# Expert loops of a two-layer network unrolled, with the token gather inside the loop and more weight slots

## The reference

```python
def expert_choice_ffn(h, w_router, w1, w3, w2):          # h: (1, 256, 1024)
    cap = (EC_CAPACITY_FACTOR * T) // N_EXPERTS          # 32 tokens per expert, 16 experts
    aff = softmax(h @ w_router)
    gate, idx = top_k(swapaxes(aff, 1, 2), cap)
    xe = h[bidx, idx]
    hid = silu(einsum('becd,edf->becf', xe, w1)) * einsum('becd,edf->becf', xe, w3)   # w1, w3: 1024 x 1024 per expert
    ye = einsum('becf,efd->becd', hid, w2) * gate        # w2: 1024 x 1024 per expert
    return zeros_like(h).at[bidx, idx].add(ye)
for l in range(2):
    h2 = rms_norm(x, norm_ffn[l]) * (1 + sc2) + sh2
    x = x + g2 * expert_choice_ffn(h2, ...)
    if l == 0:                                           # the context stream, with the same weights
        xc = xc + g2c * expert_choice_ffn(hc2, ...)
```

## Time and profile before

| | us |
|---|---|
| median of 3 runs (2080.01 to 2083.17) | 2082.44 |
| the profiled execution | 2084.03 |
| its span, first to last instruction | 2082.2 |
| PE busy in the span | 1763.1 (85%) |
| DVE, ACT, POOL busy | 605.1, 333.9, 124.7 |
| longest part of the chain that ended last | L603 on PE 55%, DMA of in_moe 19% |
| mean granted PE clock | 0.943 |

### The profile page before, as it was taken

One profiled execution on the slowest core, in us unless ns is written; L12 is line 12 of the kernel. 1 busy time (PEld: TensorE's weight loads), 2 busy tenths in 40 slices (PEclk: granted clock), 3 DMA queues, 4 the chain that ended last, 5 costly groups with the idle time before them and its releaser, 6 DMA issues.

```text
span 2082.2 us, 22735 instructions
## 1 busy us (share of the span) xinstructions
PE 1763.1 (85%) x9074; PEld 857.0 (41%) x9074; DVE 605.1 (29%) x1359; ACT 333.9 (16%) x717; POOL 124.7 (6%) x176
## 2 busy tenths in 40 slices
PE   6999999899999998899998888989998655555655
PEld 3844544444444575433332222346564322222222
DVE  2157827742200583421111111130343100010101
ACT  2112222211101462110000000021331000000000
POOL 0000112340100000000000000000000000000000
PEclk9999999999999999999999999999999888787877
DMA  8241238775422102339999999941313899999996
GB/s 322 101 162 67 96 144 302 268 277 218 161 81 81 41 1 81 122 125 430 429 429 428 428 428 428 428 208 52 136 74 128 370 428 428 428 429 428 428 428 279
DMA packets 39058, 537.57 MB, mean 258 GB/s; under 512 B 4330, under 2 KB 4714, under 8 KB 6612
## 3 DMA queue, kind: packets, MB, share of 16 engines
q1 hardware_dynamic: 37860, 530.85, 61.6%
q0 software_dynamic: 1136, 5.88, 0.8%
HBM read 535.66 MB, written 1.05 MB: 258 GB/s over the span
## 4 chain that ended last, share of the span: by engine, by line
PE 58%; DMA 21%; issue 13%; DVE 4%; POOL 2%; ACT 1%; DVEq 1%; POOLq 1%; SPq 0%; ACTq 0%
PE bank L603 55%; DMA mem<-in_moe 19%; PE bank L613 2%; DVE mem L1277 1%; DMA mem<-in_w_ada 1%; DVEq L1274 1%; PE bank L610 1%; POOL mem L2234 0%; DMA mem<-in_ada_w 0%; POOL mem L2222 0%; POOLq L2223 0%; POOL mem L2225 0%; DVE mem L1720 0%; ACT mem L1874 0%; POOL mem L2216 0%
## 5 line engine op out<-in xcount | busy, mean ns | idle before, releaser
L603 PE MATMUL bank<-mem 128*32 128x256 f32 (+9 forms) x8390 | 1662.0, 504 | 280.0 <-DMA mem<-in_moe 178.3
L603 PEld LDWEIGHTS bank<-mem 128*32 128x32 f32 (+3 forms) x8390 | 779.8, 155 | 1114.7 <-issue 768.6
L1720 DVE TENSOR_TENSOR mem<-mem,bank 128x512 f32<-128x512 f32 (+1 forms) x32 | 17.8, 555 | 480.9 <-PE bank L603 480.9
L1917 ACT ACTIVATE mem<-bank 128x512 f32<-128x512 f32 (+5 forms) x183 | 95.1, 526 | 316.9 <-PE bank L603 300.9
L1874 ACT ACTIVATE mem<-bank 128x256 f32<-128x256 f32 (+3 forms) x98 | 41.8, 444 | 561.3 <-PE bank L613 390.9
L1723 DVE TENSOR_TENSOR mem<-bank,mem 32x256 f32<-32x256 f32 (+1 forms) x96 | 48.9, 510 | 281.4 <-PE bank L603 280.6
L613 PE MATMUL bank<-mem 128*128 128x128 f32 x624 | 96.7, 283 | 29.6 <-DVE mem L1720 21.3
L613 PEld LDWEIGHTS bank<-mem 128*128 128x128 f32 x624 | 72.6, 147 | 84.3 <-DVE mem L1720 46.1
L2100 ACT ACTIVATE mem<-bank 128x512 f32<-128x512 f32 (+1 forms) x32 | 15.7, 491 | 444.4 <-PE bank L603 444.4
L1414 DVE SCALAR_TENSOR_TENSOR mem<-mem 128x256 f32<-128x256 f32 x160 | 82.2, 514 | 9.6
L1277 DVE TENSOR_SCALAR mem<-bank,mem 128x256 f32<-128x256 f32 (+2 forms) x148 | 62.4, 482 | 45.0 <-PE bank L603 42.2
(11 more groups left out here) (182 smaller groups left out, 543.1 us busy)
## 6 DMA issues: line engine op xcount, KB each, us to landing
mem<-in_moe SPq DMA_DIRECT2D x192, 2048.0 KB, 25.2
mem<-in_ada_w SPq DMA_DIRECT2D x24, 2048.0 KB, 8.5
mem<-in_w_in SPq DMA_DIRECT2D x10, 2048.0 KB, 7.6
mem<-in_w_ada SPq DMA_DIRECT2D x6, 2048.0 KB, 12.9
mem<-in_even_w_in SPq DMA_DIRECT2D x6, 2048.0 KB, 10.6
mem<-in_w_out SPq DMA_DIRECT2D x4, 2048.0 KB, 8.5
mem<-in_odd_w_in SPq DMA_DIRECT2D x3, 2048.0 KB, 24.5
mem<-in_even_w_out SPq DMA_DIRECT2D x2, 2048.0 KB, 8.2
```

Of the source, the lines that this page charges most:

```text
L603: return nc.tensor.matmul(o, lhsT, rhs, start=start, stop=stop, skip_group_check=True)
L1917: took(name, S.activation(o, i, func))
```

## The change

It does five things at once. The expert loops are written out, and their tiles go through the bank rotation. Token rows aren't gathered for all experts in `route`: `gather(e + 1)` selects 32 tokens of every stream and feature part with 32 stationary one-hot columns (4 column groups side by side), ACT copies it to xg, PE transposes it (`gather_T`), and DVE applies scale and shift (`modulated`) into one of two xe_stg buffers, all in expert e's turn. y rows of four experts of a stream share 128 partitions, so the scatter comes once in four experts in both layers; its matrix dgT is built by `slot_rows` from copies of sel_e and aff_rows spread with identity columns. Layer 0 has 8 weight slots and layer 1 has 9: slot 6 is the start of ARENA1, 7 is hT, 8 is the context half of xres; pieces take them in turn. The first 8 or 9 issues wait for named tiles (`before`), the others for the slot's last piece. POOL has no part in the loops. Small buffers move to make room (res_2, x_rows for layer 1, hid, hidT, silu_h and dgT into gate_mix[0], xe_stg into tri_f and tri_b), and `route` loses its gather, its second `warm` and d_tok, and gains two copies into aff_rows.

```diff
+        PIECES = 6 * EXPERTS
+        moe_slots = [[turn % 3, 3, 4, 6, (turn + 1) % 3, (turn + 2) % 3, 5, 7]]
+        for i in range(PIECES):
+            put(f"m0.{i}", moe_slots[0][i % 8])
...
+        moe_slots.append([turn % 3, 3, 4, 5, 6, 8, (turn + 1) % 3, (turn + 2) % 3, 7])
+        for i in range(PIECES):
+            put(f"m1.{i}", moe_slots[1][i % 9])
+        SLOT_AT = [RING0 + SLOT * i for i in range(6)] + [ARENA1, HT, XRES + 2048]
...
+                S = P // n_grp
...
+                def piece(e, j):
+                    n = f"m{l}.{6 * e + j}"
+                    pe.wait_ge(filled[place[n]], 16 * fill_no[n])
+                    return slot(place[n], 4, D)
+                def half_done(e, j, last):
+                    last.then_inc(half_used, 1)
...
+                def gather(e):
+                    t = B.open(f"g{l}.{e}", "act")
+                    pe.wait_ge(d_ready, EXPERTS * l + e + 1)
+                    for q in range(2):
+                        for i, (s, h) in enumerate(m["parts"]):
+                            last = mm(t.ps[32 * i:32 * i + 32, 0:W], d_e[e % 2][:, 2 * s + q, :], x_rows[l][:, 2 * s + q, W * h:W * h + W], q == 0, q == 1)
+                    B.close(t, last)
...
+                def gather_T(e):
+                    wait_took(pe, f"g{l}.{e}")
+                    t = B.open(f"x{l}.{e}", "dve")
+                    for j in range(J):
+                        last = tr(t.ps[:, P * j:P * j + P], xg[:, P * j:P * j + P])
+                    B.close(t, last)
+                def up(e, i, by):
+                    t = B.open(f"h{i}{l}.{e}", by)
+                    for half in range(2):
+                        w = piece(e, 2 * i + half)
+                        for q in range(4):
+                            kt = 4 * half + q
+                            for g in range(n_grp):
+                                last = mm(t.ps[S * g:S * g + S, 0:W], xe_stg[e % 2][:, kt, 0:S], w[:, q, W * g:W * g + W], kt == 0, kt == KT - 1)
+                        if half == 0:
+                            half_done(e, 2 * i, last)
+                    B.close(t, last)
...
+                def down(e):
+                    t = B.open(f"y{l}.{e}", "dve")
+                    wait_took(pe, f"ht{l}.{e}")
+                    for half in range(2):
+                        w = piece(e, 4 + half)
+                        for q in range(4):
...
+                                last = mm(t.ps[S * g:S * g + S, 0:W], hT4[:, ft % J, ft // J, :], w[:, q, W * g:W * g + W], ft == 0, ft == 7)
+                        if half == 0:
+                            half_done(e, 4, last)
+                    B.close(t, last)
+                    done_with(f"m{l}.{6 * e + 5}")
+                def slot_rows(b):
+                    for s in range(m["streams"]):
+                        t = B.open(f"bs{l}.{b}{s}", "dve")
+                        rows = slice(32 * s, 32 * s + EXPERTS)
+                        for half, src in enumerate((sel_e, aff_rows)):
+                            for i in range(PER):
+                                c = 32 * s + PER * b + i
+                                last = mm(t.ps[32 * i:32 * i + 32, SEQ * half:SEQ * half + SEQ], ident[rows, c:c + 1].to_broadcast([EXPERTS, CAP]), src[rows, :], True, True)
                         B.close(t, last)
...
+                def scatter(b):
+                    for s in range(m["streams"]):
+                        wait_took(pe, f"bs{l}.{b}{s}")
+                    wait_took(pe, f"y{l}.{PER * b + PER - 1}")
+                    for j in range(T):
+                        for n in range(2):
+                            t = B.open(f"sc{l}.{b}{j}{n}", "dve")
+                            B.close(t, mm(t.ps[:, :], dgT[:, j // 2, P * (j % 2):P * (j % 2) + P], y_rows[j // 2][:, 512 * n:512 * n + 512], True, True))
+                gather(0)
+                gather_T(0)
+                for e in range(EXPERTS):
+                    wait_took(pe, f"x{l}.{e}")
+                    up(e, 0, "act")
+                    if e + 1 < EXPERTS:
+                        gather(e + 1)
+                    up(e, 1, "dve")
+                    if e + 1 < EXPERTS:
+                        gather_T(e + 1)
+                    if e and e % PER == 0:
+                        scatter(e // PER - 1)
+                    if e % PER == 0:
+                        slot_rows(e // PER)
+                    wait_took(pe, f"h1{l}.{e}")
+                    t = B.open(f"ht{l}.{e}", "act")
+                    for j in range(J):
+                        last = tr(t.ps[:, P * j:P * j + P], hid[:, P * j:P * j + P])
+                    B.close(t, last)
+                    down(e)
+                scatter(EXPERTS // PER - 1)
             route(0)
             experts(0)
...
+                    last = V.tensor_copy(aff_rows[r0:r0 + EXPERTS, :], ps[r0:r0 + EXPERTS, 0:SEQ])
+                took(f"affT{l}", last)
                 ps = arrive(dve, f"slotT{l}")
                 took(f"slotT{l}", V.tensor_copy(three(slot_t), ps[:, 0:EXPERTS * T].rearrange("p (a b) -> p a b", b=EXPERTS)))
...
+                def modulated(e):
+                    ps = arrive(dve, f"x{l}.{e}")
+                    if e >= 2:
+                        dve.wait_ge(mm_done, tiles[f"h1{l}.{e - 2}"].no)
+                    both = lambda a: a.rearrange("p (k i) -> p k i", i=2)
+                    if l == 0:
+                        src = ps.rearrange("p (j s h c) -> p j s h c", s=2, h=2, c=CAP)
+                        dst = xe_stg[e % 2].rearrange("p (h j) (s c) -> p h j s c", h=2, c=CAP)
+                        by = lambda a, h: both(a)[:, 4 * h:4 * h + 4, :].unsqueeze(3).to_broadcast([P, 4, 2, CAP])
+                        todo = [(dst[:, h], src[:, :, :, h, :], by(norm_a[:, NORM_A[n], :], h), by(ada_col[sh][:, v, :], h)) for h in range(2)]
+                    else:
+                        src = ps[:, 0:256].rearrange("p (j h c) -> p h j c", h=4, c=CAP)
+                        dst = xe_stg[e % 2].rearrange("p (h j) c -> p h j c", h=4)[:, :, :, 0:CAP]
+                        by = lambda a: both(a)[:, :, 0].rearrange("p (h j) -> p h j", h=4).unsqueeze(3).to_broadcast([P, 4, 2, CAP])
+                        todo = [(dst, src, by(norm_a[:, NORM_A[n], :]), by(ada_col[sh][:, v, :]))]
+                    for o, i, a, _ in todo:
+                        V.tensor_tensor(o, i, a, ALU.mult)
+                    settle()
+                    for o, _, _, b in todo:
+                        last = V.tensor_tensor(o, o, b, ALU.add)
+                    took(f"x{l}.{e}", last)
...
+                def sums(b):
+                    for j in range(T):
+                        for h in range(2):
+                            ps = arrive(dve, f"sc{l}.{b}{j}{h}")
+                            x = xres[:, j, 512 * h:512 * h + 512]
+                            took(f"sc{l}.{b}{j}{h}", V.tensor_tensor(x, x, ps[:, :], ALU.add))
...
+                def one_hot(e):
+                    if e >= 2:
+                        dve.wait_ge(mm_done, tiles[f"g{l}.{e - 2}"].no)
+                    V.tensor_tensor(d_e[e % 2][:, 0:T, :], C("iota").unsqueeze(1).to_broadcast([P, T, CAP]),
+                                    slot_t[:, 0:T, e:e + 1].to_broadcast([P, T, CAP]), ALU.is_equal).then_inc(d_ready, 1)
+                settle()
+                one_hot(0)
+                one_hot(1)
+                modulated(0)
+                for e in range(EXPERTS):
+                    ps = arrive(dve, f"h1{l}.{e}")
+                    wait_took(dve, f"h0{l}.{e}")
+                    if e:
+                        dve.wait_ge(mm_done, tiles[f"ht{l}.{e - 1}"].no)
+                    took(f"h1{l}.{e}", V.tensor_tensor(hid[:, 0:W], silu_h[:, 0:W], ps[:, 0:W], ALU.mult))
+                    if e + 1 < EXPERTS:
+                        modulated(e + 1)
+                    if e + 2 < EXPERTS:
+                        one_hot(e + 2)
+                    if e and e % PER == 0:
+                        sums(e // PER - 1)
+                    if e % PER == 0:
+                        for s in range(m["streams"]):
+                            ps = arrive(dve, f"bs{l}.{e // PER}{s}")
+                            V.tensor_scalar(dgT[:, s, :], ps[:, 0:SEQ], C("iota_p"), None, ALU.is_equal)
+                            settle()
+                            took(f"bs{l}.{e // PER}{s}", V.tensor_tensor(dgT[:, s, :], dgT[:, s, :], ps[:, SEQ:2 * SEQ], ALU.mult))
+                    ps = arrive(dve, f"y{l}.{e}")
+                    r0 = CAP * (e % PER)
+                    for i in range(4):
+                        s, h = (i % 2, i // 2) if l == 0 else (0, i)
+                        last = V.tensor_tensor(y_rows[s][r0:r0 + CAP, W * h:W * h + W], ps[CAP * i:CAP * i + CAP, 0:W], gate_ffn[l][CAP * i:CAP * i + CAP, :], ALU.mult)
+                    took(f"y{l}.{e}", last)
+                sums(EXPERTS // PER - 1)
             route(0)
             experts(0)
```

(75 more changed lines are left out.)

249 lines of the change are left out of this document (42 added, 207 removed).

## The result

| | us |
|---|---|
| changed kernel, median of 4 runs (2027.07 to 2032.93) | 2029.90 |
| kernel before, runs beside it | 2081.23 |
| ratio after / before, 95% interval | 0.9757 [0.9733, 0.9781] |
| profiled execution: its time, its span | 2027.07, 2025.3 |

51.3 us were gained, where 55.8 had been forecast. The page's rate row, which answers to the earlier trace rows. The plateaus are now 427 to 428, and the last slice ahead of each is fuller than before: slice 17, counted from 0, has 299 GB/s for 125, and slice 30 has 332 for 128.

What follows compares the result with a forecast made beforehand. Weight transfers were taken to bound both expert loops. Layer 0's 30.6 us and layer 1's 26.7, less 1.5 for code, gave 55.8 off the median 2082.4: 2026.6 us, range 2018 to 2044.

Steps and rivals of the forecast that it cites:

- What bounds it: Both expert loops: each runs at the pace of its weights, 29.3 us an expert at 429 GB/s.
- 1, the gather leaves the gap: Ahead of the loops: first expert matmul 25.2 us earlier in layer 0, 13.0 in layer 1.
- rival C: Layer 0's gather and slot_rows: column groups don't overlap, 33.6 us an expert, sum about 2116; chance 0.04.
- 2, clock: Loop starts: TensorE's clock may fall while it idles, costing 2 us in layer 0 and 1 in layer 1.
- 3, slots: Before the loops: 88 and 87 pieces remain instead of 90, saving 9.8 and 14.7 us.
- rival D: SyncE's in-order issues hold early pieces into the loop, leaving only the earlier start: 2051, or no change; chance 0.03.
- 4, a full queue: In the loops: layer 0 has a bubble taken as 1 us, layer 1 none; weights still decide by 13 us.
- the thirteenth: Layer 0's loop: sign that TensorE should wait for DMA from about the thirteenth expert.
- 5, tails: After the last landing: layer 0's y has four operations instead of two, +1.4 us; layer 1's tail same in count.
- 6, straight code: Unrolled loops: code fetched during the plateaus, some 60 more packets or 1 MB, taken as 1.5 us.
- The sign that I had named for this error: In the loops: a plateau below 425 GB/s would show the straight-code cost mis-sized.
- rival A: Both loops: the weight queue stays the bound from an earlier start, span 2019 to 2034; chance 0.77.

Runs made afterwards that it cites:

- Late start: Changed kernel with unneeded matmuls before gather(0), 29 of 128x512 in layer 0 and 15 in layer 1: 2064.50 us, 0.9917 of before.
- six slots: Changed kernel with the old six weight slots in each layer, all else as changed: 2059.03 us, 0.9887 of before.
- more code on TensorE: Changed kernel with 64 one-column matmuls behind each of layer 1's first 15 experts: 2035.89 us, 0.9783 of before.

## Why the prediction was right, point by point

- **What bounds it: right.** Both loops run at the weights' pace. Late start and six slots moved the end by at least what they were worth (34.6 for 34.9, and 29 for 24.4).
- **1, the gather leaves the gap: right.** TensorE's first expert matmul came 25.7 (885.40 - 797.20 = 88.2 after aT0, against 113.9) and 13.7 us earlier, for 25.2 and 13.0. The four column groups overlap, so rival C was wrong.
- **2, clock: right.** It fell to 0.50 in both layers in this profile and cost 1.6 and 1.6 us (taken: 2 and 1).
- **3, slots: right.** 9.6 and 14.8 us for 9.8 and 14.7; rival D was wrong.
- **4, a full queue: right in its result, wrong in two sizes.** There was no bubble, where 1 us was taken: the last piece's first share landed 432.68 us after the first release, and 432.6 is before's 442.39 less two pieces. The slack on TensorE was 25 us, not 13. I had measured to the landing instead of to the end of the half-piece behind it (3.7 us); TensorE's own work is 421 us long instead of 425; and the landing is some 5 later after the loop's start than in the 13, by the clock and the code. TensorE first waited for a weight in the ninth expert, not the thirteenth. I had spread the scatters evenly, but only one stands ahead of the ninth expert.
- **5, tails: right.** y took 2.80 us instead of 1.39, and where the clock stays up the stretch to bT0 is 188.5 against 187.0 in five profiles. The further 1.6 in this profile is what is left of half clock in the scatter (1.7) and in the transposes behind it (another 1.6): against the changed kernel's second profile, 1.6 of the 3.3 are gone again some 120 us further on, and the rest stays.
- **6, straight code: the term that was mis-sized.** I had 1.5 us, from 1 MB at the whole queue's 428 GB/s. It costs 3.1 and 4.1: 437.22 - (443.91 - 2 x 4.89) and 434.03 - (444.61 - 3 x 4.89). The spread of the last piece's raises grew by the same, from 1.48 to 4.50 and from 2.24 to 6.31. The number of packets had been put too high, at some 60: TensorE has 16 and 27 code packets in the two loops, where it had 1 and 5. The price of one was wrong by more. The work of bringing a block isn't shared by sixteen engines: GpSimd's blocks made one engine late, TensorE's a group of eight, and a weight piece has landed only when the latest engine has brought its part. The 15 and 22 additional packets of TensorE cost the landing 3.1 / 15 = 0.21 and 4.1 / 22 = 0.19 us each, and so did the 15 that the run with more code on TensorE added, 3.1 us or 0.21 each. The sign that I had named for this error, a plateau below 425 GB/s, did not come: the plateaus were at 427 and 428, as the earliest engines kept their pace. "DMA: Bandwidth & Descriptors" of the Trainium skill, section "Queues, rings and completion order", says that a DMA engine serves its queue rows in turn, one packet at a time. That code makes an engine's weights late fits this; the turn by packets itself no run shows. "Runtime: NRT & Kernel Launch" of the Trainium skill, section "Instruction fetch mechanics", says that the fetch is mostly hidden. For TensorE the trace agrees: in layer 0's loop its waits for anything but a weight are 0.73 us in each expert, with none above 0.8. But here the weights' landing pays for it, with 3.1 and 4.1 us.

The low end of rival A was added up wrongly: with clock and bubble at 0, 3 and 1 us off 2026.6 give 2022.6; 2021.1 has the code's 1.5 in it already, and "code and start costs at their lowest" takes it off once more.

The sum, from the forecast's 55.8: start +1.2, clock -0.1, slots -0.1, y -0.1, code and bubble together -4.7 (7.2 for 2.5), half clock behind layer 0 -1.6. Of the -4.7, the code is -5.7 and the missing bubble +1.0. That is 50.4, and with the 1.2 by which the tail happened to be shorter 51.6 of the 51.7 in the profiles; the medians give 51.3.

That the forecast came within 4.5 us is in part luck: the late engines cost 5.7 us more than summed, and the start, 1.2 us earlier, and the missing bubble gave 2.2 back.

What stays open: by which rule an engine's code blocks are given to DMA engines, one for GpSimd and eight for TensorE; why GpSimd's packets cost 0.46 to 0.54 us each and not 0.31; and why the beginning of the kernel, which no edit touched, varies by 12 us between executions.

## What to carry to other kernels

When a stretch runs at the pace of its transfers, find the idle gap ahead of it: what pays is each further piece that lands in the gap and each microsecond by which the first buffer is released sooner, and both could be read off SyncE's issues to within 1 us. Moving work from the gap into the loop is free as long as the compute engine's total, with its uneven parts put where they fall, stays under the transfer time. Unrolled code isn't free beside a saturated queue: count its packets, and price them against the few DMA engines that bring them, not against all sixteen.

## What the runs showed of the hardware that was not expected

- 7200 instructions of straight code on an engine that nobody waits for made the kernel 33 us slower, and the same instructions in a loop 0.
- The rate stays at 427 of 428 GB/s while one engine falls behind by 13 to 16 us, some three pieces of 4.89 us, by which the other fifteen run ahead into free slots. A rate doesn't show a late engine; the 25 to 33 GB/s at the end and the sixteen raises of a piece's semaphore do.
- The clock at a border of the same kernel fell in one profile and not in another (scatter 8.81 and 7.12 us).
